# Three of the 24 modulation chunks are weighed on VectorE and only summed on TensorE

## The reference, cut to what matters

```
mod = jax.nn.silu(cvec) @ w_mod[l] + b_mod[l]
sh1, sc1, g1, sh2, sc2, g2 = jnp.split(mod[:, None, :], N_MOD, axis=-1)
h = rms_norm(x, norm_mix[l]) * (1.0 + sc1) + sh1
out = mixer(h)
x = x + g1 * out
h = rms_norm(x, norm_ffn[l]) * (1.0 + sc2) + sh2
x = x + g2 * hier_moe(h, ...)
```

## Time and profile before

| | |
|---|---|
| three runs | 798.5, 799.91, 800.84 us (median 799.91) |
| profiled execution, its own time | 800.09 us |
| its span in the trace | 798.3 us |
| TensorE busy | 734.6 us (92%) |
| VectorE busy | 313.3 us (39%) |
| ScalarE, GpSimd busy | 162.9 us, 18.1 us |
| moved by the DMA engines | 291.48 MB, 365 GB/s in the mean |

### The profile page before, as it was taken

How to read it: one execution, slowest core, us unless ns; L and a number is a source line. 1 busy time by engine, 2 the same in 40 slices (tenths; PEclk the granted TensorE clock), 3 DMA queues, 4 the chain that set the end, 5 groups by cost and what they waited for, 6 DMA issues and landing times.

```text
span 798.3 us, 15682 instructions
## 1 busy us (share of the span) xinstructions
PE 734.6 (92%) x6783; PEld 484.7 (61%) x6783; DVE 313.3 (39%) x684; ACT 162.9 (20%) x319; POOL 18.1 (2%) x29
## 2 busy tenths in 40 slices
PE   3999999998899999999968799999999999994977
PEld 2788467677799655655534244689865555552434
DVE  1144668572514633334430241233553334433124
ACT  3113231233211411111110032040231111111103
POOL 0000001011210000000000000001000000000000
PEclk9999999999999999999997999999999999998988
DMA  9999979496899899999999999999689999999991
GB/s 340 387 371 381 350 263 352 163 324 220 244 379 416 347 421 420 410 422 420 421 422 414 400 386 385 387 407 399 256 317 423 400 420 420 420 421 422 412 383 61
DMA packets 90647, 291.48 MB, mean 365 GB/s; under 512 B 11769, under 2 KB 14927, under 8 KB 73167
## 3 DMA queue, kind: packets, MB, share of 16 engines
q1 hardware_dynamic: 79728, 284.32, 91.1%
q10 hardware_dynamic: 10847, 6.12, 2.6%
HBM read 288.32 MB, written 2.10 MB: 364 GB/s over the span
## 4 chain that ended last, share of the span: by engine, by line
PE 79%; SPq 8%; DMA 5%; DVE 4%; ACT 3%; issue 2%; ACTq 0%; DVEq 0%
PE psum L1436 9%; PE psum L1426 8%; PE psum L933 7%; PE psum L1451 7%; PE psum L1486 7%; SPq L769 7%; PE psum L1352 5%; PE psum L1012 5%; PE psum L882 5%; PE psum L1497 4%; PE psum L1627 3%; PE psum L1645 3%; PE psum L1077 2%; DMA ring<-in_w_exp_up 2%; DMA scratch<-in_w_exp_up 2%
## 5 line engine op out<-in xcount | busy, mean ns | idle before, releaser
L1436 PE MATMUL psum<-ring,hT 128*32 128x512 f32 (+1 forms) x304 | 74.3, 615 | 11.9 <-DMA scratch<-in_w_exp_up 11.9
L1436 PE MATMUL psum<-scratch,hT 128*32 128x512 f32 (+1 forms) x368 | 74.3, 619 | 10.8 <-DMA ring<-in_w_exp_up 10.8
L1426 PE MATMUL psum<-scratch 128*128 128x128 f32 x640 | 75.5, 276 | 0.0
L1426 PEld LDWEIGHTS psum<-scratch 128*128 128x128 f32 x640 | 73.2, 192 | 1.7 <-issue 1.7
L933 PE MATMUL psum<-hT,ring 128*128 128x256 f32 x256 | 57.8, 382 | 1.1 <-DVE hT L2192 0.6
L933 PEld LDWEIGHTS psum<-hT,ring 128*128 128x128 f32 x256 | 47.8, 190 | 9.6 <-DVE hT L2192 2.0
L1497 PEld LDWEIGHTS psum<-const,scratch 128*128 128x128 bf16 x432 | 40.5, 97 | 17.9 <-issue 12.9
L1497 PE MATMUL psum<-const,scratch 128*128 128x256 bf16 x432 | 50.4, 272 | 0.0
L2644 DVE TENSOR_SCALAR hT<-psum,const 128x512 f32<-128x512 f32 x20 | 15.0, 750 | 85.7 <-PE psum L1486 84.2
L2009 ACT ACTIVATE scratch<-psum 128x256 f32<-128x256 f32 x20 | 7.7, 385 | 199.3 <-PE psum L1436 122.8
L1436 PEld LDWEIGHTS psum<-scratch,hT 128*32 128x32 f32 (+1 forms) x368 | 20.4, 118 | 41.5 <-issue 41.5
(11 more groups left out here) (357 smaller groups left out, 987.6 us busy)
## 6 DMA issues: line engine op xcount, KB each, us to landing
ring<-in_w_mod SPq DMA_DIRECT2D x40, 1024.0 KB, 11.8
scratch<-in_w_exp_down SPq DMA_DIRECT2D x32, 1024.0 KB, 17.5
ring<-in_w_exp_down SPq DMA_DIRECT2D x24, 1024.0 KB, 18.0
scratch<-in_w_exp_gate SPq DMA_DIRECT2D x22, 1024.0 KB, 17.1
scratch<-in_w_exp_up SPq DMA_DIRECT2D x22, 1024.0 KB, 19.2
ring<-in_w_exp_gate SPq DMA_DIRECT2D x18, 1024.0 KB, 17.5
ring<-in_w_exp_up SPq DMA_DIRECT2D x18, 1024.0 KB, 20.0
scratch<-in_w_exp_gate SPq DMA_DIRECT2D x24, 512.0 KB, 9.6
```

Of the source, the lines that this page charges most:

```text
L1426: last = mm(bank[b][:, k * P:(k + 1) * P], hrow[:, t, half * 4 + k, :], Pm[:, t, :], start=(t == 0), stop=(t == 1))
L1436: last = mm(bank[0][i * m:(i + 1) * m, :], xg[:, k, i * m:(i + 1) * m], w[e][:, k, :, :], start=(k == 0), stop=(k == KT - 1))
```

## The change

Chunks (0, 10), (1, 5) and (1, 10), listed in `SUMMED`, are weighed by VectorE first. `weigh_rows` multiplies each of the eight pieces k of 128 rows by silu(c) of its row and adds the pieces up, apart for each stream: 16 instructions of 128 x 512, two of them a product with a scalar (k = 0), 14 a product with a scalar plus a sum. The sums are written over pieces 1 and 0 of the chunk itself, and the first two of t = 0 into a spare place of `const`. What is left for TensorE is the sum over the 128 partitions: per stream and block one product with a column of ones (`chosen`), 8 instead of 32. A new semaphore, `v_acc`, counts VectorE's steps; TensorE waits for it ahead of the 8 products.

Placement: (0, 10) is weighed in three parts, k = 0 to 2 after `later_values(1)`, k = 3 to 5 after the mixed rows of t = 0, k = 6 and 7 ahead of `shift_row`. (1, 5) and (1, 10) follow `norm(3, 1, 0)`, ahead of the centring. TensorE's products for (1, 5) move from before `("in1", 3)` to behind it, and `mod_turn` and `modulation` of that group move behind `("in1", 0)`. The load of (1, 10) moves ahead of those of `("in1", 0)`, `("in1", 1)` and `("out1", 0)`. Two semaphores are merged with others.

```diff
+SUMMED = [(0, 10), (1, 5), (1, 10)]
...
         put("in1", 2)
+        put("in1", 3)
         put_mods(1, 5)
-        for j in (3, 0, 1):
+        for j in range(2):
             put("in1", j)
...
+        middle = [index[s] for s in (("mod", 1, 4), ("in1", 2), ("mod", 1, 5), ("in1", 3), ("mod", 1, 10), ("in1", 0),
+                                     ("in1", 1), ("out1", 0), ("out1", 1), ("mod", 1, 11))]
+        loaded = list(range(moe_at[0], moe_at[0] + MOE_SLOTS)) + middle + list(range(moe_at[1], len(stream) + 3))
...
+                if (l, j) in SUMMED:
+                    pe.wait_ge(S.v_acc, 2 * KT * (SUMMED.index((l, j)) + 1))
+                    for t in range(NB):
+                        for m in range(4):
+                            last = mm(bank[mbank[g]][32 * m:32 * m + NB, at:at + P], chosen[t], w[:, 1 - t, m * P:(m + 1) * P],
+                                      start=(t == 0), stop=(t == NB - 1))
+                    used(last)
+                    return
...
+            def weigh_rows(l, j, k0=0, k1=KT):
+
+                w = slot_kn(chunk_full(dve, ("mod", l, j)))
+                done = 2 * KT * SUMMED.index((l, j))
+                early = part(E0 + 8704, (512,)) if (l, j) in ((0, 6), (0, 8)) else const[:, C_LEV:C_LEV + 512]
+                for k in range(k0, k1):
+                    for t in range(NB):
+                        out = early if t == 0 and k < 2 else w[:, 1 - t, :]
+                        if k == 0:
+                            if t == 1:
+                                dve.wait_ge(S.v_acc, done + 1)
+                            ins = V.tensor_scalar(out, w[:, k, :], condT[:, t, k:k + 1], None, ALU.mult)
+                        else:
+                            dve.wait_ge(S.v_acc, done + (4 if k == 2 else 2 * k - 1 + t))
+                            ins = V.scalar_tensor_tensor(out, w[:, k, :], condT[:, t, k:k + 1], early if t == 0 and k == 2 else out, ALU.mult, ALU.add)
+                        ins.then_inc(S.v_acc, 1)
...
             for t in range(NB):
+                weigh_rows(0, 10, 3 * t, 3 * t + 3)
                 dve.wait_ge(S.a_ors, NB + t + 1)
...
+                if l == 0:
+                    weigh_rows(0, 10, 6, KT)
                 shift_row(l)
...
             norm(3, 1, 0)
-            modulation(M_B)
+            weigh_rows(1, 5)
+            weigh_rows(1, 10)
             for t in range(NB):
                 dve.wait_ge(S.a_gv, 3 + t)
```

More of the change, by code:

```diff
@@ L270, in __init__ @@
         self.t_st = sem("t_st")
-        self.t_u = sem("t_u")
         self.t_v = sem("t_v")
@@ L280, in __init__ @@
         self.v_ab = sem("v_ab")
-        self.v_abx = sem("v_abx")
+        self.v_acc = sem("v_acc")
         self.v_att = sem("v_att")
@@ L426, in build @@
         flat = hT[:, :, :, :].rearrange("p k t n -> p (k t n)")
-        mrow = [wrt[:, :, :, :].rearrange("p l k n -> p (l k n)")[:, 0:512]] * 5 + [part(2048, (512,)), flat[:, D:D + 512], part(0, (512,)), flat[:, D:D + 512]]
+        mrow = [wrt[:, :, :, :].rearrange("p l k n -> p (l k n)")[:, 0:512]] * 5 + [part(2048, (512,)), flat[:, D:D + 512], const[:, C_LEV + 512:C_LEV + 768], flat[:, D:D + 512]]
         mbank = [7] * 6 + [5, 3, 5]
@@ L630, in build @@
             place[c], prior[c], held[at] = at, None if at >= RING else last_in[at], c
-        for c in range(moe_at[0] + len(turns), len(stream) + 3):
+        for c in loaded[len(turns):]:
             if c == moe_at[1]:
@@ L652, in build @@
             quarters.update((moe_at[l] + MOE_SLOTS - 2, moe_at[l] + MOE_SLOTS - 1))
-        for c in range(moe_at[0], len(stream)):
+        for c in loaded[:len(stream) - moe_at[0]]:
             count[slot_of(c)] += 64 if c in quarters else 16 if c in singles else 32
@@ L675, in chunk_full @@
             return slot_of(c)
+        chosen = [const[:, C_J8 - 1:C_J8 + 1], const[:, C_I32:C_I32 + 2]]
         def parts_of(n):
@@ L830, in _ @@
             moe_further(0)
-            for c in range(moe_at[0] + MOE_SLOTS, moe_at[1]):
+            for c in middle:
                 load(stream[c], "all")
@@ L877, in mod_chunk @@
                 at = (2 * nth + g if g < M_1 else nth + 2 if g in MOE_MOD else nth) * P
-                if g > M_HI and nth == 0:
+                if g > M_HI:
                     pe.wait_ge(S.v_mod, g)
+                if (l, j) in SUMMED:
[6 more added lines that the diff above has]
+                    return
                 for k in range(KT):
@@ L1618, in _ @@
             for j in range(2):
-                if j == 1:
-                    mod_chunk(1, 5)
                 s = chunk_full(pe, ("in1", 2 + j))
@@ L1630, in _ @@
                 used(last)
-            mod_turn(M_B)
+            mod_chunk(1, 5)
             for j in range(2):
@@ L1635, in _ @@
                 if j == 1:
-                    pe.wait_ge(S.v_mod, M_B + 1)
+                    mod_turn(M_B)
                     pe.wait_ge(S.ld_router, 16 * 10)
@@ L1643, in _ @@
                     b = 2 * j + m // 2
+                    if b == 3 and m == 2:
+                        pe.wait_ge(S.v_mod, M_B + 1)
                     for k in range(KT):
@@ L1647, in _ @@
                     if m == 1:
-                        last.then_inc(S.t_u, 1)
+                        last.then_inc(S.t_v, 1)
                 used(last)
@@ L1740, in mod_row @@
             def mod_row(g):
-                act.wait_ge(S.used, index[("mod",) + MODS[g][-1]] + 1)
+                act.wait_ge(S.used, max(index[("mod",) + m] for m in MODS[g]) + 1)
                 if g > 0:
@@ L1862, in _ @@
             roots()
-            act.wait_ge(S.v_abx, 1)
+            act.wait_ge(S.v_ab, 2)
             A(t16a, t16a, ACT.Exp).then_inc(S.a_e1, 1)
@@ L2073, in _ @@
                 A(vtk[:, t, j * 512:(j + 1) * 512], bank[4 + n], ACT.Gelu_apprx_tanh).then_inc(S.a_gv, 1)
-                if n == 1:
+                if n == 3:
                     mod_row(M_B)
@@ L2077, in _ @@
                 if b % 2 == 0:
-                    act.wait_ge(S.t_u, b // 2 + 1)
+                    act.wait_ge(S.t_v, 2 + b // 2 + 1)
                 else:
@@ L2267, in _ @@
             link(V.tensor_tensor(lamq, lamq, lamk, ALU.mult))
-            V.tensor_reduce(lame, lamq.rearrange("p (a n) -> p a n", a=2), AX.X, ALU.add).then_inc(S.v_abx, 1)
+            V.tensor_reduce(lame, lamq.rearrange("p (a n) -> p a n", a=2), AX.X, ALU.add).then_inc(S.v_ab, 1)
             convolve(2)
@@ L2830, in _ @@
                 V.tensor_scalar(vtk[:, t, :], vtk[:, t, :], lnm[:, t:t + 1], None, ALU.subtract).then_inc(S.v_cen, 1)
+            modulation(M_B)
             dve.wait_ge(S.a_lnr, 1)
```

## The result

The kernel before took 799.76 us (median of 8 runs), the changed kernel 804.32 (801.12 to 808.41): ratio 1.0055, 95% interval 1.0036 to 1.0073. The forecast was 795.8 us. The profiled execution took 806.75 us, 2.4 above the median; its span is 804.9.

A forecast was written before the change was run, and what follows sets the result against it. TensorE's progress through each mixer was taken to end a hole in the otherwise full DMA weight stream. Saving 4.2 us and losing 0.1 gave -4.1 us, from a median of 799.91 to 795.8 us; range 794.3 to 799.2 us.

The forecast's parts named there:

- -4.2 + 0.1: Whole kernel: three chunks save TensorE 1.39 us each, 4.2 us; waiting on VectorE in layer 0 costs 0.1 us.
- The records of a summed chunk: TensorE, mixer chunks: 16 records instead of 64, costing 0.47 us instead of 1.86 us.
- the 10.3 us of weighing: VectorE, each summed chunk: 16 instructions take 10.3 us, sums 0.67 us apart; upper bound 11.5 us.
- no wait at `v_logit`: Layer 0's output projection: VectorE is ready at about 223.8 us, TensorE asks at about 225.5, 1.7 us to spare.
- the moved loads in time: Layer 1: ("in1", 0) lands by 502.1 us, 4.6 us before TensorE needs it; the two behind have over 10 us.
- The collision with GpSimd: End of layer 0's weighing: one collision costs VectorE 0.4 to 0.8 us, so TensorE waits about 0.1 us.
- the layer 1 piece of the chain: Wait for the last expert weights of layer 1: starts 4.1 us earlier.
- Its holes: Nearly idle DMA stretches ending each mixer, at 272.5 and 568.4 us: shrink by 1.3 and 2.8 us.
- The first (layer 0's share lost): VectorE's instructions don't overlap in layer 0, `v_logit` comes 1.1 to 1.5 us late: 797.0 us; chance 0.16.
- The fourth, the slower one: VectorE bounds the end of layer 0's mixer at 1.08 us a sum; TensorE waits 5.3 us: 801.0 us; chance 0.06.
- I am wrong if: Refuting signs: holes don't shrink although TensorE is early, or TensorE waits for `v_acc` or ("in1", 0).
- rival D: Raised after the measurement, no chance given: the router's weights load, 1.17 us late at 227 us, starts the loss.

The follow-up runs named there:

- the short branch: Changed kernel with the never-run loop over further expert tiles left out of TensorE's program in layer 0's rare branch: 798.16 us, again 797.12 us.
- both remedies: Changed kernel without the 11 `v_mod` waits, and its jump stall avoided by padding (796.01 us) or by leaving out layer 0's never-run loop (796.10, 795.74 us).
- the parts alone: Kernel before with only chunk (0, 10) weighed: ratios 1.0000 and 0.9983; with only (1, 5) and (1, 10) weighed: 796.77 us, ratio 0.9981.

## Why the prediction was wrong

1. **The step that failed is the sum, -4.2 + 0.1**, made of durations and waits alone. It had no term for where the removed instructions put the rest of TensorE's program. The 96 that chunk (0, 10) loses, less 10 added waits, moved one jump by 86; that costs 7.1 us in the trace. Leaving only the landing place of the jump different gives 798.16 and 797.12 us (ratios 0.9995 and 0.9974) in place of 804.32 and 805.28 (1.0055 and 1.0060). That is shown, and so is that the jump waits for a packet of the program. That the sequencer asks for a block on entering the one before fits every row of the table and is argued, not seen. The Trainium skill (Runtime: NRT & Kernel Launch, "Instruction fetch mechanics") says that a taken branch whose target lies outside the two blocks at hand forces a fetch before execution goes on. The packet of 16 KB ahead of 476.3 us agrees. The same section says that fetching is otherwise hidden by the rate of issue; the pieces on L1091, 1.38 and 1.48 us in the changed kernel, speak against it for short instructions.

2. **The diff's 11 waits on `v_mod` have no term in the prediction.** Seven of them lie ahead of 163 us in the trace. Behind them TensorE runs short instructions (233 records of 64 x 64 and as many weight loads from 172.97 to 180.61 us, so 256 instructions in some 4 us), and pieces of waiting for the program stand in every trace (2.4 us before, 3.7 after). With the short branch or padding alone the time is 797.1 to 798.2 us, with the waits out too 795.7 to 796.1. Of that the pieces show 0.7 us in the first pair (3.1 against 2.4 us, with L1148) and nothing in the second (2.9 against 2.9); where the rest goes stays open.

3. **What was right.** The records of a summed chunk, its 1.31 us, the 10.3 us of weighing (from 491.47 to 501.79 us in the changed kernel), the 0.67 us between sums, no wait at `v_logit`, the moved loads in time. Starts 0.66 us apart with durations of 0.75 also speak against what the prediction cited from the Trainium skill (VectorE: DVE Perf Modes, "The DRAIN you can't avoid"), that an instruction starts only when the pipeline is empty; the prediction left out that the same paragraph excepts an instruction that nothing holds back. The collision with GpSimd was priced at 0.4 to 0.8 us and cost VectorE 0.34. The changed kernel with both remedies is the kernel that the forecast spoke of: 796.01, 796.10 and 795.74 us, forecast 795.8. How close it comes is in part luck: each interval is 3 to 4 us wide, and the parts alone gave about 0.5 and 1.9 us, 2.4 of the 4.1. In one of its profiles the layer 1 piece of the chain starts 3.2 us earlier than in the earlier trace rows (2.3 and 4.1 in the other two), 4.1 were forecast:

```profile
751.50 15.64 DMA ring<-in_w_exp_up
```

   Its holes, to be held against the earlier trace rows (the windows lie 1 and 2 us earlier), have shrunk, the second to a share of 0.27 in 7 us:

```profile
271.50:275.00 3.50, 3.50 (x36) 2.30 (x24) 1.25 (x8) 0.17 (x1) 0.00 (x0) 1.00 0.44 138
276.00:566.00 290.00, 270.99 (x1936) 166.24 (x1929) 112.98 (x192) 47.23 (x97) 2.52 (x6) 0.98 1.02 408
566.40:573.40 7.00, 6.80 (x70) 5.98 (x70) 5.81 (x20) 2.94 (x8) 0.00 (x0) 1.00 0.27 77
```

   Windows that hold a whole hole tell more. From 262 to 282 us the DMA share is 0.88 before, 0.90 to 0.92 in the three profiles with both remedies, and 0.91 and 0.93 with chunk (0, 10) alone: 2.4 us empty before, 1.4 to 2.0 then. The first hole shrank by 0.4 to 1.0 us, 1.3 were forecast. From 550 to 592 us the share is 0.75 before and 0.79 to 0.83 with both remedies, 1.7 to 3.4 us less of a hole, 2.8 forecast; but it is 0.75 and 0.80 in the two profiles of chunk (0, 10) alone, so one profile is worth some 2 us here.

4. **The rivals.** The first (layer 0's share lost) came in part, as far as the two runs of that chunk alone can tell, but not through its mechanism: VectorE's instructions do overlap, and `v_logit` was in time. The fourth, the slower one, was a wrong mechanism with the right sign; a stall of VectorE was priced to 1.08 us an instruction, measured were 0.67. The tests named as "I am wrong if" (holes, `v_acc`, ("in1", 0)) would not have found the cause, since they look only at what the diff touches.

5. **The router's weights** (rival D). The wait of 1.17 us at 227 us is in 9 of the 16 profiles, with 0.5 to 1.5 us, in two of them without any part of the change; it is a scatter of that load's landing, of which the changed kernel's profile had its share. In the kernel before with products as padding it costs double, since the granted clock is 0.83 in the 10 us behind it (the 64 records of the output projection took 8.90 us there, 7.41 without); behind waits of 1.45 us in two other profiles they took 7.41:

```profile
PE psum L1305 <- DMA wrt<-in_w_router_expert: 1.4, 1, 1.4
```

## What to carry to other kernels

An edit that adds or removes instructions moves all that follow on their engine against the 16 KB blocks in which the program is fetched; where a jump soon follows the start of a block and lands in the next one, that can cost more than the edit gains (7.1 us here, against a gain of some 4). So look in the profile for idle time with no waiter behind a branch and for the branch's own duration before believing or rejecting a change of under 1%, and try the change once more with the never-run body shortened or some 80 instructions of padding placed where the engine waits anyway. Be wary of adding waits that are always fulfilled to a stretch of short TensorE instructions; here they probably cost 1.4 to 1.8 us.

## What was not expected of the hardware

A jump record of TensorE takes 0.24 to 0.45 us with its target at hand and, in these runs, 0.8 to 6.3 us without it, under a DMA load of 386 GB/s. It ends 2.4 to 2.6 us after the packet starts. The 4.8 us of standing also cost the clock: 0.51 of full speed for the next 5.7 us, 2.2 us lost. A standing of only 2.4 us, in the run with 40 instructions of padding, was followed by the same slow rows (1.46 us for the three idle products instead of 0.82):

```profile
472.02 1.46 PE L1313 MATMUL psum<-zeros 32*128 32x512 bf16 x3 [2.39 <-issue]
```

An already fulfilled wait instruction on TensorE costs about 16.2 / 170 = 0.095 us in a row of them, three times the 0.029 us of a chunk's record with its weight load. And GpSimd's four instructions of 128 x 32 take 3.08 us beside VectorE's sums, where they took 1.61 alone:

```profile
231.19 3.08 POOL L2145 TENSOR_TENSOR scratch<-wrt,mulA 128x32 f32<-128x32 f32 x4
```
